# An expert layer whose rows are gathered pair by pair, with a longer weight ring and single buffers

## The chip, the cores and the metric

One core of one Trainium2 chip runs the whole program. The time is the device time of that core in microseconds; three runs are given and their median is used. Smaller is better.

## The reference

Two transformer-like blocks run one after the other on 256 tokens of width 1024. The change lies in the last part of the second block, a mixture of experts with 32 experts of inner width 256, two of them per token, and in the norm behind it:

```
g_logits = t @ w_rg + b_rg;  g_sel = argmax(g_logits)           # 4 groups
e_in = (t @ w_re + b_re) of the chosen group                    # 8 experts each
top_v, top_i = top_k(e_in, 2);  w_top = softmax(top_v) * g_w
act = silu(t @ w_gate[e]) * (t @ w_up[e]) * combine[t, e]
y = sum over e of act @ w_down[e];   h = h + y
out = rms_norm(h, norm_final)
```

The reference computes every expert for every token and multiplies by a combine weight that is zero for 30 of the 32. The kernel computes only the chosen ones.

## The kernel before

The program is written out by hand for each engine, and semaphores tie the engines together. The dense layers before the experts read 112 weight units of 1 MB (`raw`), which ScalarE and GpSimd split in a high and a low part (`whi`, `wlo`, lines 580 and 524); that part is as before. The last unit is the router's (`rt`, lines 2305 to 2313).

Behind the router, VectorE finds the two experts of each token and makes one-hot masks `oh` and their sum `msum` (line 1623). TensorE turns them into counts (`cn`) and positions (`ds`). The 512 choices (256 tokens, two each) are sorted by expert: a choice's position is its expert's offset plus its rank there. VectorE makes a 256x512 selection matrix `pick`, and TensorE gathers all 512 rows of the normed tokens at once, transposed, with the high and low parts `xnh` and `xnl` as stationaries (`xg`, lines 2341 to 2347). ScalarE copies them out as `xs`.

The experts' work is cut into tiles of TS = 32 positions of one expert. Two tiles make a pair. 16 pairs ("e") hold the first tile of each of the 32 experts, and 8 pairs ("o") can hold the tiles of experts with more than 32 choices; which experts these are is known at run time only. `pair_plan` (line 117) sets the order of the 24 pairs. For each pair GpSimd copies the two windows of `xs` into `xw` (line 547) and of the choice weights into `wx`. TensorE runs `gate_up` (line 2381: 32 matmuls with 32-column stationaries, four side by side on the array), two transposes of the gated product (`act_transposed`, line 2373), `down` (line 2400) and `combine` (line 2412), which adds each row back to its token in four PSUM banks that stay occupied through all pairs. ScalarE applies silu and copies the high part of y (`y_hi`), VectorE multiplies gate and up (`gate`), copies the activations (`act_copy`), makes the owner matrix `sT` (`owners`) and the low part of y (`y_lo`). Everything there is in two buffers, and the order on TensorE is gate_up(j), combine(j-2), down(j-1), with the transposes of pair j-1 in the middle of gate_up(j).

Expert weights come in units of 1 MB through a ring of NRING = 13 buffers. A pair needs six units: four for gate and up (part 0 and 1), two for down (part 2). SyncE issues them in the order of `ring_plan` (line 129). The first four go to memory that is free once the output projection of the mixer is done. The next nine wait for the last dense weights to be used (line 505). From then on each entry waits until the entry that held its buffer has been read (line 508). For an "o" pair the load is conditional and moves nothing when there is no such tile.

Of the kernel before, what the change touches and what calls it, by code (L numbers as in the profile page):

```python
# [34 lines left out]
NRING = 13  # L35
# [6 lines left out]
for _n, _w in (("ident", 128), ("tri", 128), ("stri", 128), ("ones", 128), ("cmpmask", 30), ("cos", 16), ("sin", 16),  # L42
               ("invf", 16), ("iota", 32), ("rcos", 128), ("rsin", 128), ("negmask", 128), ("slot", 1)):
    CONST[_n] = (sum(w for _, w in CONST.values()), _w)
# [72 lines left out]
def pair_plan():  # L117

    pairs = []
    for n in range(NEXP // 2):
        pairs.append(("e", n))
        if n % 2 == 0 and n or n == 3:
            pairs.append(("o", len(pairs) - n - 1))
    return pairs


def ring_plan(npair):


    ring = []
    for j in range(npair + 1):
        if j < npair:
            ring += [(j, part, u) for part in range(2) for u in range(2)]
        if j:
            ring += [(j - 1, 2, u) for u in range(2)]
    return ring


def bank_plan(units):
# [58 lines left out]
    G += [("xg", k) for k in range(8)]  # L200
# [24 lines left out]
    W += [("rtt", 0), ("cn", 0), ("ds", 0), ("wr", 0), ("pT", 0), ("od", 0)]  # L225
# [12 lines left out]
def program(nc, x_d, mem_d, pos_d, cst_d, sml_d, dec_d, npost_d, nfin_d, w_d, ew_d, out_d):  # L238
# [9 lines left out]
    NT = len(PAIRS)  # L248
    RING = ring_plan(NT)
    ENTRY = {u: n for n, u in enumerate(RING)}  # L250
    ctx = ExitStack()
    with ctx:
# [128 lines left out]
        xnh = at("xnh", A + 8 * KB, [P, TT, DM], f32r)  # L381
        xnl = at("xnl", A + 16 * KB, [P, TT, DM], f32r)
        pick = at("pick", A + 24 * KB, [P, TT, NSLOT], f32r)
        ramp = at("ramp", A + 28 * KB, [P, NSLOT])
        a = A + 30 * KB
        oh = at("oh", a, [P, 2, TT, 32])
        msum = at("msum", a + 512, [P, TT, 32])
        prod = at("prod", a + 768, [P, 2, TT, 32])
        cnt = at("cnt", a + 1280, [32, P])
        offn = at("offn", a + 1792, [P, 2, 32])  # L390
        row = at("row", a + 2048, [P, 8, 32])
        over = at("over", a + 3072, [P, 8, NOVER])
        posf = at("posf", a + 3584, [P, 4])
        start = at("start", a + 3616, [P, NEXP + NOVER], i32)
        mine = at("mine", a + 3840, [P, NPAIR])
        overi = at("overi", a + 4064, [P, 2, NOVER], i32)
        rtl = at("rtl", A + 38 * KB, [P, 8, TT * 36])
        lgt = at("lgt", A + 38 * KB + 2304, [36, S])
        flt = at("flt", A + 42240, [32, P])
        xw = at("xw", A + 42 * KB, [P, 2, 8, 2 * TS])  # L400
        sg = at("sg", A + 46 * KB, [P, 2, 256])

        yhl = at("yhl", A + 8 * KB, [P, 2, 2, 512], f32r)
        ac = at("ac", A + 28 * KB, [2 * TS, 2, 256])
        tally = at("tally", A, [P, 2, NEXP])
        match = at("match", A + 512, [P, NOVER, NEXP])
        mval = at("mval", A + 512 + 2 * KB, [P, NOVER, NEXP])
        vals = at("vals", A + 512 + 4 * KB, [P, 4, NEXP])
        aT = at("aT", A + 22 * KB, [P, 2, 4 * TS])
        nfin = at("nfin", A + 24 * KB, [P, DM])  # L410
        xs = at("xs", base + 9 * UW * 4, [P, 8, NSLOT])
        a = base + 9 * UW * 4 + 16 * KB
        posT = at("posT", a, [P, 2 * S])
        sT = at("sT", a + 2 * KB, [P, 2, S], f32r)
        wrow = at("wrow", a + 4 * KB, [P, NSLOT])
        wx = at("wx", a + 6 * KB, [P, 2, 2 * TS])
        wpick = at("wpick", a + 8 * KB, [P, TT, NSLOT])
        diag = at("diag", a + 12 * KB, [P, 4, P])
        wtmp = at("wtmp", a + 14 * KB, [P, NSLOT])
# [2112 lines left out]
```

## Time and profile before

| | |
|---|---|
| time, median of 3 runs | 1198.32 us (1196.86 to 1198.56) |
| the profiled execution | 1198.53 us |
| its span | 1196.7 us |
| TensorE matmul busy | 1023.9 us, 86% |
| VectorE, ScalarE, GpSimd busy | 619.5, 426.6, 612.6 us |
| gate/up matmuls (L2393), 1536 records | 103.6 us |
| down matmuls (L2409), 384 records | 49.0 us |
| combine matmuls (L2419), 96 records | 32.4 us |
| expert weight issues (L507, L515) | 144, of 1024 KB each |

The span runs from the first to the last instruction; the time of an execution includes what lies around it. A record is what the profiler writes for one pass of an instruction; a plain fp32 matmul has two, an fp32r one has one. Busy times of TensorE overlap from one record to the next, so that the pace of a stretch is read from start to start. The experts' stage is about the last 285 us. All times below are counted from the start of the span.

### The profile page before, as it was taken

The page shows a single profiled execution, that of the slowest core. Times are in us where ns is not written, and L with a number is a line of the kernel's source. Part 1 is how long each engine was busy: PE and PEld are TensorE (multiplying, and loading weights), DVE is VectorE, ACT ScalarE, POOL GpSimd, SP SyncE. Part 2 cuts the span into 40 slices and gives each one's busy share as a digit, 9 for nine tenths or more (in the row PEclk, how much of TensorE's full clock was granted, in tenths as well). Part 3 has the DMA queues.
Part 4 walks back from the last instruction along what each step waited for, and adds up shares of the span by engine and source line. Part 5 has one row for each costly group of instructions (what it writes and reads, how often), then busy time and mean ns, then how long its engine had stood idle before and what let it go on. Part 6 is the DMA issues. An engine that isn't in the chain of part 4 may idle for free.

```text
span 1196.7 us, 19506 instructions
## 1 busy us (share of the span) xinstructions
PE 1023.9 (86%) x7452; PEld 840.0 (70%) x7452; DVE 619.5 (52%) x1343; ACT 426.6 (36%) x637; POOL 612.6 (51%) x549
## 2 busy tenths in 40 slices
PE   5897899987957979999999999999985879787773
PEld 4786788987946869999977789898964534333331
DVE  6303246368545665554159986842116656444445
ACT  4543333332224545554434344344432311111111
POOL 5997814456748676664765349888540011110100
PEclk9999898999987889999999999999996879999996
DMA  6554522333334344332433226554434589999990
GB/s 251 172 204 160 192 71 71 100 131 123 140 107 141 139 143 141 139 121 96 145 137 106 97 81 211 176 172 170 155 138 189 234 340 413 420 421 420 420 398 36
DMA packets 31907, 224.90 MB, mean 188 GB/s; under 512 B 3664, under 2 KB 3664, under 8 KB 5072
## 3 DMA queue, kind: packets, MB, share of 16 engines
q1 hardware_dynamic: 30672, 220.07, 48.9%
q10 hardware_dynamic: 1152, 3.67, 0.9%
q8 instruction: 59, 0.97, 0.3%
q14 instruction: 24, 0.20, 0.0%
HBM read 273.01 MB, written 1.05 MB: 229 GB/s over the span
## 4 chain that ended last, share of the span: by engine, by line
POOL 44%; issue 31%; DMA 12%; PE 9%; DVE 3%; SPq 0%; ACT 0%; POOLq 0%; DVEq 0%
POOL wlo L524 44%; DMA ring<-in_experts 12%; PE ps L2393 3%; PE ps L2409 1%; PE ps L2419 1%; DVE yhl L1720 1%; PE ps L2345 0%; PE ps L2346 0%; PE ps L1807 0%; PE ps L1809 0%; PE ps L1808 0%; PE ps L2378 0%; POOLq L527 0%; DVE x L1782 0%; SPq L507 0%
## 5 line engine op out<-in xcount | busy, mean ns | idle before, releaser
L524 POOL TENSOR_TENSOR wlo<-raw,whi 128x512 fp32r<-128x512 f32 x448 | 583.6, 1336 | 308.4 <-ACT whi L580 307.9
L1857 PE MATMUL ps<-xhi,whi 128*128 128x256 f32 x960 | 283.6, 295 | 10.5 <-DVE xlo L1210 4.1
L1858 PE MATMUL ps<-xhi,wlo 128*128 128x256 f32 x960 | 277.7, 289 | 0.0
L1859 PE MATMUL ps<-xlo,whi 128*128 128x256 f32 x960 | 277.4, 289 | 0.0
L580 ACT ACTIVATE whi<-raw 128x2048 fp32r<-128x2048 f32 x112 | 214.0, 1914 | 147.0 <-PE ps L1859 75.2
L1857 PEld LDWEIGHTS ps<-xhi,whi 128*128 128x128 f32 x960 | 191.0, 199 | 14.7 <-issue 7.1
L1858 PEld LDWEIGHTS ps<-xhi,wlo 128*128 128x128 f32 x960 | 190.6, 199 | 1.0 <-issue 0.7
L1859 PEld LDWEIGHTS ps<-xlo,whi 128*128 128x128 f32 x960 | 190.4, 198 | 0.0
L2393 PE MATMUL ps<-ring,xw 128*32 128x256 f32 x1536 | 103.6, 407 | 33.0 <-DMA ring<-in_experts 32.3
L1807 PE MATMUL ps<-whi,xhi 128*128 128x512 f32 (+3 forms) x298 | 117.8, 395 | 13.1 <-POOL wlo L524 11.1
L547 POOL COPY xw<-xs 128x256 f32 x48 | 20.4, 452 | 209.9 <-PE ps L2393 162.7
L1808 PE MATMUL ps<-wlo,xhi 128*128 128x512 f32 (+3 forms) x298 | 114.9, 386 | 0.0
L1809 PE MATMUL ps<-whi,xlo 128*128 128x512 f32 (+3 forms) x298 | 114.6, 385 | 0.0
L2393 PEld LDWEIGHTS ps<-ring,xw 128*32 128x32 f32 x1536 | 52.7, 114 | 77.3 <-issue 58.3
L1720 DVE TENSOR_TENSOR yhl<-ps,yhl 32x512 fp32r<-32x512 f32 x96 | 65.9, 687 | 75.9 <-ACT yhl L910 74.8
L1807 PEld LDWEIGHTS ps<-whi,xhi 128*128 128x128 f32 x298 | 57.6, 193 | 26.6 <-POOL wlo L524 10.5
L1808 PEld LDWEIGHTS ps<-wlo,xhi 128*128 128x128 f32 x298 | 57.6, 193 | 10.7 <-issue 1.0
L1809 PEld LDWEIGHTS ps<-whi,xlo 128*128 128x128 f32 x298 | 57.6, 193 | 10.3
L1150 DVE TENSOR_REDUCE stat<-ps 128x1 f32<-128x128 f32 (+1 forms) x36 | 11.0, 306 | 90.0 <-PE ps L1918 69.7
L2409 PE MATMUL ps<-ring,aT 128*32 128x512 f32 x384 | 49.0, 629 | 9.6 <-issue 6.8
L903 ACT ACTIVATE sg<-ps 128x256 f32<-128x256 f32 x24 | 9.2, 384 | 119.2 <-PE ps L2393 119.2
L658 ACT ACTIVATE pr<-ps,stat 128x128 f32<-128x128 f32 x64 | 26.2, 415 | 55.8 <-DVE stat L1151 55.8
(465 smaller groups left out, 1496.0 us busy)
## 6 DMA issues: line engine op xcount, KB each, us to landing
ring<-in_experts SPq DMA_DIRECT2D x144, 1024.0 KB
raw<-in_weights SPq DMA_DIRECT2D x112, 1024.0 KB, 4.9
x<-in_x SPq DMA_DIRECT2D x2, 512.0 KB, 4.5
memt<-in_mem ACTq DMA_DIRECT2D x1, 1024.0 KB, 6.0
out<-xn ACTq DMA_DIRECT2D x4, 256.0 KB, 2.5
decay<-in_decay ACTq DMA_DIRECT2D x1, 512.0 KB, 4.1
npost<-in_norm_post ACTq DMA_DIRECT2D x1, 512.0 KB, 5.4
nfin<-in_norm_final ACTq DMA_DIRECT2D x1, 512.0 KB, 8.1
```

What stands on the lines that cost most here:

```text
L524: ins = pool.tensor_tensor(wlo[:, j, c], raw[:, j, c], whi[:, j, c].bitcast(f32), ALU.subtract)
L580: act.activation(whi[:, n % NSPL, :], raw[:, n % NRAW, :], ACT.Copy).then_inc(hi_ready, 1)
L658: ins = act.activation(p_buf[:, c], pj((S_, u))[:, c], ACT.Exp, bias=stat[:, NMAX + k + t:NMAX + k + t + 1], accum_out=stat[:, sums + k + ...
L1720: ins = v.tensor_tensor(yhl[other, j % 2, b, :], ps[3][own, :], yhl[own, j % 2, b, :].bitcast(f32), ALU.subtract)
L1807: mm(out, lh, rh, start=first, stop=False, skip_group_check=skip)
L1808: mm(out, lh, rl, start=False, stop=False, skip_group_check=skip)
L1809: return mm(out, ll, rh, start=False, stop=last, skip_group_check=skip)
L1857: mm(o_, wh[:, k, cc], hi[:, k0 + r0 + k, :], start=first, stop=False, skip_group_check=True)
L1858: mm(o_, wl[:, k, cc], hi[:, k0 + r0 + k, :], start=False, stop=False, skip_group_check=True)
L1859: ins = mm(o_, wh[:, k, cc], lo[:, k0 + r0 + k, :], start=False, stop=last, skip_group_check=True)
L2393: ins = mm(ps[j % 2][q:q + TS, 0:256], xw[:, j % 2, 4 * part + k, TS * u:TS * u + TS], wt[u][:, k, 256 * h:256 * h + 256], start=first, st ...
L2409: ins = mm(ps[3][q:q + TS, :], aT[:, j % 2, 2 * TS * k + TS * u:2 * TS * k + TS * u + TS], wt[u][:, k, 512 * h:512 * h + 512], start=k == ...
```

## The change

1. Slots are numbered by expert and rank. The slot of a choice is 32 times its expert plus its rank; a choice of rank 32 or more goes to an overflow slot, which needs the tallies of all experts (`tally`) first. Pair 0 needs only the ranks.
2. The gather of all rows, `xs`, `xnh`, `xnl` and GpSimd's window copies go. Each pair has a `gather(j)` on TensorE: 16 fp32 matmuls with `xn` as stationary and a 256x64 selection `pick` as moving operand. VectorE makes the selection (`pick_rows`), and scales and copies the rows out (`rows_out`).
3. The choice weights are no longer applied to the activations. They are gathered once into `wslot`, a weight per slot and pair, and scale y on its way out of PSUM (`y_hi`, `y_lo`).
4. The ring has 18 buffers and a plain order, and each buffer of the dense layers is handed over by its own last reader.
5. The buffers of gate/up, transposes, `sg`, `ac`, `aT` and `yhl` are single. TensorE's order is gate_up(j), gather(j+1), transposes of j, combine(j-1), down(j).
6. The residual `x` is added by TensorE into the four combine banks (`residual_in`), once. The final squares read PSUM directly.
7. Two overflow pairs stand elsewhere in the order of pairs; there are still 24.

The diff, cut to its core:

```diff
-NRING = 13
+NRING = 18
@@ pair_plan
-        if n % 2 == 0 and n or n == 3:
+        if n in (3, 4, 5, 7, 9, 11, 13, 14):
@@ ring_plan
-    ring = []
-    for j in range(npair + 1):
-        if j < npair:
-            ring += [(j, part, u) for part in range(2) for u in range(2)]
-        if j:
-            ring += [(j - 1, 2, u) for u in range(2)]
-    return ring
+    return [(j, part, u) for j in range(npair) for part in range(3) for u in range(2)]
@@ ring buffers
+        slots = [A + (48 + 8 * i) * KB for i in range(4)]
+        slots += [base + 8 * KB * i for i in (1, 2, 0)]
+        slots += [base + 8 * KB * i for i in (4, 7, 5, 8)] + [base + 80 * KB, base + 96 * KB, A + 40 * KB]
+        slots += [base + 8 * KB * i for i in (3, 6)] + [base + 72 * KB, base + 88 * KB]
@@ SyncE
-                if n == 4:
+                if 4 <= n < 7:
+                    sp.wait_ge(lo_ready, NU - 6 + n)
+                if n == 7:
+                    sp.wait_ge(weights_used, NU - 1)
+                if n == 14:
                     sp.wait_ge(weights_used, NU)
@@ ScalarE
             for j in range(NT):
                 silu(j)
-                if j:
-                    y_hi(j - 1)
...
+                if j == 0:
+                    copy(("pT", 0), posT[:, :])
+                    wait_done(act, ("ws", 0))
+                y_hi(j)
@@ VectorE
+            def pick_rows(j, at_):
+                do(v.tensor_tensor(hit[:, :, :], C("iota").unsqueeze(1).to_broadcast([P, 4, 2 * TS]), ALL4(at_, 2 * TS), ALU.is_equal))
+                sync()
+                v.tensor_tensor(pick[:, j % 2, :, :], hit[:, 0:2, :], hit[:, 2:4, :], ALU.add).then_inc(sem("pick_ready"), 1)
+
+            def rows_out(j):
+                dve.wait_ge(sem("gathered"), j + 1)
+                v.tensor_tensor(xw[:, j % 2, :, :], ps[1][:, :].rearrange("p (k s) -> p k s", k=8),
+                                D("g_moe").unsqueeze(2).to_broadcast([P, 8, 2 * TS]), ALU.mult).then_inc(sem("rows_ready"), 1)
...
             for j in range(NT):
-                gate(j)
                 if j:
                     y_lo(j - 1)
-                owners(j)
+                gate(j)
+                if j + 1 < NT:
+                    rows_out(j + 1)
                 act_copy(j)
                 if j == 0:
-                    overflow()
+                    slot_weights()
+                    wait_full(dve, ("ws", 0))
+                    release(v.tensor_copy(wslot[:, :], pj(("ws", 0))[:, 0:NPAIR]), ("ws", 0))
+                    wait_done(dve, ("ws", 0))
+                    further()
+                    wait_done(dve, ("pT", 0))
+                owners(j)
+                if j + 2 < NT:
+                    pick_rows(j + 2, codes[:, PLACE[j + 2], :])
@@ TensorE
+            def gather(j):
+                pe.wait_ge(sem("pick_ready"), j + 1)
+                for k in range(8):
+                    for t in range(TT):
+                        ins = mm(ps[1][:, 2 * TS * k:2 * TS * k + 2 * TS], xn[:, t, k * P:k * P + P], pick[:, j % 2, t, :], start=t == 0, stop=t == 1)
+                ins.then_inc(sem("gathered"), 1)
...
-            gate_up(0)
-            for j in range(1, NT):
+            for j in range(NT):
                 gate_up(j)
-                if j >= 2:
-                    combine(j - 2)
-                down(j - 1)
-            act_transposed(NT - 1)
-            combine(NT - 2)
-            down(NT - 1)
+                if j == 0:
+                    code_rows()
+                if j + 1 < NT:
+                    gather(j + 1)
+                act_transposed(j)
+                if j == 0:
+                    weights_of_slots()
+                if j == 1:
+                    residual_in()
+                if j:
+                    combine(j - 1)
+                down(j)
             combine(NT - 1)
```

How this moves instructions is seen in the order of each engine. First TensorE before, in the second half of the pairs: the end of one pair's gate/up (`ring_170`, `ring_171` are ring buffers) and what follows it.

```order
L2393 MATMUL ps<-ring_170,xw 32x256 [waits ring_loaded12,ring_loaded11]
L2378 MATMUL ps<-cst,ac 128x64 [waits aT_ready,gated]
L2378 MATMUL ps<-cst,ac 128x64
L2393 MATMUL ps<-ring_170,xw 32x256 x2
L2393 MATMUL ps<-ring_171,xw 32x256 x2
L2419 MATMUL ps<-yhl,sT 128x512 [waits y_lo_ready,owners_ready]
L2419 MATMUL ps<-yhl,sT 128x512 x3
L2409 MATMUL ps<-ring_159,aT 32x512 [waits aT_ready,y_lo_ready,ring_loaded1,ring_loaded0]
```

The same place in the changed kernel, where L2349 is gate/up, L2293 the gather, L2336 the transposes, L2377 combine and L2361 down:

```order
L2349 MATMUL ps<-ring_168,xw 32x256 x2
L2349 MATMUL ps<-ring_169,xw 32x256 x2
L2293 MATMUL ps<-pick,xn 128x64 [waits pick_ready]
L2293 MATMUL ps<-pick,xn 128x64 x15
L2336 MATMUL ps<-cst,ac 128x64 [waits gated]
L2336 MATMUL ps<-cst,ac 128x64
L2377 MATMUL ps<-yhl,sT 128x512 [waits y_lo_ready,owners_ready]
L2377 MATMUL ps<-yhl,sT 128x512 x3
L2361 MATMUL ps<-ring_170,aT 32x512 [waits aT_ready,ring_loaded17,ring_loaded16]
```

The transposes belonged to the pair before and stood inside gate/up; now they are the pair's own, and 16 full-width matmuls stand ahead of them. Down is that of the same pair, no longer of the one before.

SyncE's queue where the ring is first filled, before (every row is one unit; rows without a wait follow at once, four, nine and then one by one):

```order
L507 DMA ring_159<-in_experts 128x2048 [waits weights_used]
L507 DMA ring_163<-in_experts 128x2048 [waits weights_used]
L507 DMA ring_159<-in_experts 128x2048 [waits first_used]
L507 DMA ring_160<-in_experts 128x2048 [waits first_used]
L507 DMA ring_161<-in_experts 128x2048 [waits gu_full]
```

And now:

```order
L511 DMA ring_154<-in_experts 128x2048 [waits weights_used]
L511 DMA ring_158<-in_experts 128x2048 [waits lo_ready]
L511 DMA ring_161<-in_experts 128x2048 [waits weights_used]
L511 DMA ring_168<-in_experts 128x2048 [waits weights_used]
L511 DMA ring_154<-in_experts 128x2048 [waits first_used]
L511 DMA ring_156<-in_experts 128x2048 [waits gu_full]
L511 DMA ring_158<-in_experts 128x2048 [waits y_full]
```

Four units go on the first wait, three on a wait each for the splits, seven on the next and four on the last before reuse begins with the nineteenth.

VectorE between the slot weights of pair 0 and the low part of its y, in the changed kernel; `which_slot` feeds the matmuls of `weights_of_slots`, `mval`, `match` and `over` are the overflow table, `pick` is what gather(2) waits for:

```order
L1702 TENSOR_TENSOR which_slot<-islot,choice 128x512 [waits islot_ready]
L1705 COPY which_pair<-which_pair 128x4 [waits which_ready,dve_step]
L1734 COPY wslot<-ps 128x24 [waits bank_full6]
L1711 TENSOR_TENSOR mval<-cst,tally 128x512 [waits bank_done6]
L1713 TENSOR_TENSOR match<-mval,tally 128x512 [waits dve_step]
L1715 SCALAR_TENSOR_TENSOR match<-mval,match 128x512 [waits dve_step]
L1717 TENSOR_REDUCE over<-match 128x16 [waits dve_step]
L1669 TENSOR_SCALAR own<-posT,cst 128x512 [waits bank_done5]
L1671 TENSOR_TENSOR sT<-own 128x256 [waits dve_step]
L1599 TENSOR_TENSOR pick<-hit 128x128 [waits dve_step]
L1678 SCALAR_TENSOR_TENSOR yhl<-ps,wslot,yhl 32x512 [waits y_hi_ready]
```

Before, the overflow table stood between the activations' copy of pair 0 and the gate of pair 1, and nothing of the next rows hung on VectorE.

## Rows read from the trace of the kernel before

**Rows 1.** Stretches: length; busy PE PEld DVE ACT POOL; PEclk, DMA share, GB/s.
```profile
890.00:900.00 10.00, 10.00 (x43) 8.19 (x42) 4.19 (x13) 1.15 (x2) 2.47 (x2) 0.93 0.00 0
920.00:930.00 10.00, 6.88 (x23) 5.94 (x23) 6.38 (x27) 0.69 (x1) 0.00 (x0) 0.50 1.01 425
950.00:960.00 10.00, 4.19 (x66) 2.05 (x54) 9.40 (x27) 0.97 (x2) 1.04 (x4) 0.81 0.18 75
1130.00:1140.00 10.00, 6.96 (x62) 3.04 (x66) 2.80 (x7) 0.46 (x2) 1.04 (x4) 0.83 1.01 419
613.90:616.00 2.10, 2.10 (x19) 2.04 (x18) 0.00 (x0) 0.60 (x1) 1.91 (x2) 1.00 0.60 254
```

**Rows 2.** The weights' DMA queue: packets, MB, share of 16 engines.
```profile
q1 hardware_dynamic: 30672, 220.07, 48.9%
```

**Rows 3.** SyncE in order of time: start us, us, what.
```profile
912.48 32.15 SPq L507 DMA_DIRECT2D ring<-in_experts  x12
```

**Rows 4.** Waits from 965 to 1166 us: total us, times, longest.
```profile
PE ps L2393 <- DMA ring<-in_experts: 32.3, 18, 3.0
```

**Rows 5.** TensorE in order of time, one pair: start us, us, instruction, records.
```profile
984.06 1.20 PE L2419 MATMUL ps<-yhl,sT 128*128 128x512 f32 x4
985.19 1.93 PE L2409 MATMUL ps<-ring,aT 128*32 128x512 f32 x16
986.93 2.77 PE L2393 MATMUL ps<-ring,xw 128*32 128x256 f32 x48
989.63 0.33 PE L2378 MATMUL ps<-cst,ac 64*128 64x64 f32 x2
989.90 1.07 PE L2393 MATMUL ps<-ring,xw 128*32 128x256 f32 x16
991.23 0.47 PE L2419 MATMUL ps<-yhl,sT 128*128 128x512 f32 x1 [0.26 <-DVE yhl L1720]
```

**Rows 6.** TensorE in order of time, in the scan.
```profile
614.00 1.89 PE L2226 MATMUL ps<-xtok,segM 128*128 128x64 f32 x16
615.73 0.65 PE L2209 MATMUL ps<-segR,cst 128*128 128x512 f32 x1
```

**Rows 7.** The chain that ended last, from router to pair 0: start us, us.
```profile
919.08 1.06 PE ps L2327 x4
...
921.13 0.85 PE ps L2334 x4
...
926.52 0.77 PE ps L2345
927.29 0.43 PE ps L2346
...
932.64 0.23 PE ps L2345
...
940.59 0.42 PE ps L2393 x3
```

**Rows 8.** VectorE in order of time, positions of the choices.
```profile
923.44 0.29 DVE L1628 TENSOR_TENSOR prod<-oh,ps 128x128 f32<-128x128 f32 x1 [2.98 <-PE ps L2337]
```

**Rows 9.** Groups of VectorE from 900 us on: busy us, mean ns, idle before.
```profile
L1720 DVE TENSOR_TENSOR yhl<-ps,yhl 32x512 fp32r<-32x512 f32 x96 | 65.9, 687 | 75.9 <-ACT yhl L910 74.8
L1695 DVE TENSOR_TENSOR ac<-sg,ps 32x256 f32<-32x256 f32 x48 | 20.1, 418 | 25.2 <-ACT sg L903 24.5
L1752 DVE TENSOR_TENSOR mval<-match,vals 128x512 f32<-128x512 f32 x3 | 2.1, 689 | 0.1
```

**Rows 10.** The chain's last part: last y, last combine, first residual adds.
```profile
1178.73 0.60 ACT yhl L909
1179.33 0.50 ACT yhl L910
...
1182.79 2.06 PE ps L2419 x4
1184.87 2.48 DVE x L1782 x4
```

More of the change, by code:

```diff
@@ L248, in program @@
     NT = len(PAIRS)
+    PLACE = [n + NEXP // 2 * (kind == "o") for kind, n in PAIRS]
     RING = ring_plan(NT)
@@ L412, in program @@
[L412 to L419, printed above, removed]
-        ring = [at(f"ring{i}", A + (48 + 8 * i) * KB if i < 4 else base + (i - 4) * UW * 4, [P, UW])[:, :] for i in range(NRING)]
+        a = [A + 8 * KB]
@@ new lines, in small @@
+        def small(name, shape, dt=f32):
+            size = (4 * int(np.prod(shape[1:])) + 31) // 32 * 32
+            if a[0] <= A + 40 * KB < a[0] + size:
+                a[0] = A + 80 * KB
+            t = at(name, a[0], shape, dt)
+            a[0] += size
+            return t
+        rtl = small("rtl", [P, 8, TT * 36])
+        lgt = at("lgt", a[0], [36, S])
+        sg = small("sg", [P, 256])
+        yhl = small("yhl", [P, 2, 512], f32r)
+        oh = small("oh", [P, 2, TT, NEXP])
+        msum = small("msum", [P, TT, NEXP])
@@ new lines, in program @@
+        upto = small("upto", [P, 4, NPAIR + 1])
+        which_pair = small("which_pair", [P, 4, NPAIR])
+        which_slot = at("which_slot", a[0], [P, 4, P])
+        sT = small("sT", [P, 2, S], f32r)
+        islot = small("islot", [P, P])
+        diag = at("diag", a[0], [P, 4, P])
+        own = small("own", [P, 2 * S])
+        wslot = small("wslot", [P, NPAIR])
+        hit = small("hit", [P, 4, 2 * TS])
+        pick = small("pick", [P, 2, TT, 2 * TS])
+        posT = small("posT", [P, 2 * S])
@@ L885, in _ @@
             hi_parts("m", 8, 0, D("g_moe"))
-            for t in range(TT):
-                act.activation(xnh[:, t, :], xn[:, t, :], ACT.Copy).then_inc(sem("xnh_ready"), 1)
             act.wait_ge(sem("router_arg"), 1)
@@ new lines, in _ @@
+            do(v.tensor_scalar(flt[:, :], cnt[:, :], float(TS), None, ALU.is_gt))
+            for q in range(2, NSTEP + 1):
+                sync()
+                ins = v.scalar_tensor_tensor(flt[:, :], cnt[:, :], float(TS * q), flt[:, :], ALU.is_gt, ALU.add)
+                if q < NSTEP:
+                    do(ins)
+            ins.then_inc(sem("more_ready"), 1)
+            rows_out(0)
+            wait_full(dve, ("od", 0))
+            release(v.tensor_copy(tally[:, :, :], pj(("od", 0))[:, 0:64].rearrange("p (a e) -> p a e", a=2)), ("od", 0))
```

367 lines of the change are left out of this document (133 added, 234 removed).

## The prediction

> **What bounds the kernel now.** I read the table of stretches first. While the last dense layers run (890 to 900 us) no byte moves; at 920 to 930 the expert weights come at full rate, at 950 to 960 at 75 GB/s, and at 1130 to 1140 the DMA share is 1.01 at 419 GB/s with TensorE 0.70 busy [rows 1]. The weight queue carried 220.07 MB [rows 2]: 112 dense units and 96 expert units of 1.0486 MB are 218.1 of it. So only the 16 pairs of own tiles move weights; the 8 overflow pairs move none, but TensorE computes all 24 alike. A unit at 419 GB/s takes 2.5 us, a pair of six 15.0. Four units are fetched early, the next when the router's weights are read, at 912.5 us [rows 3]. From 965 to 1166 us TensorE waits 32.3 us for ring slots [rows 4]. Last, one pair whose weights were in time, TensorE alone [rows 5], from start to start: combine 1.13 us, down 1.74, 48 gate/up records 2.70, transposes 0.27, 16 more records 1.33 of which 0.26 is a wait: 6.91 without it. 24 x 6.91 = 166 us of TensorE stand against 16 x 15.0 = 240 us of DMA. The DMA bounds this stage, and TensorE has 74 us to spare.
>
> **The DMA side of the change** gets better. Entries 4 to 6 go out when the last splits are done, 7 to 13 when the last dense unit but the router's has been read, about 900 us, 14 to 17 at 912.5. Seven at 2.5 us from 900 are in by 917.5, four more by 927.5: the first three pairs. This moves the end only as long as the DMA bounds.
>
> **The TensorE side** gets worse. The gather of all rows at once (32 fp32r matmuls of 512 columns, 926.5 to 936.8 us) goes, and each pair gets 16 fp32 matmuls with a 128x128 stationary and 64 moving columns. An fp32 matmul is two records here (a pair's 32 gate/up matmuls show as 48 + 16). The scan has the same form: 16 records start at 614.00 us, the next group at 615.73 [rows 6], at clock 1.00 [rows 1]: 0.108 us a record. A gather is 32 x 0.108 = 3.46 us, a pair 6.91 + 3.46 = 10.4, and 24 pairs 249 us. That is more than 240 us of weights of which more come early, so TensorE becomes the bound.
>
> By the Trainium skill, "TensorE: Matmul & The Clock Gate", the section on LDWEIGHTS, a load costs by its columns, some 107 ns for 128; the row's 0.108 agrees, and the sum would be the same.
>
> Does the gather cover anything? It stands where the transposes wait for silu and gate, some 1.5 us. The old order covered those with the next pair's gate/up, so nothing is won.
>
> Do the other engines keep up, with each buffer single now? Counted from the end of a down: ACT's two y_hi end at +1.2 [rows 10], DVE's four y_lo of 0.69 [rows 9] at +4.1. Gate/up ends at +3.6, silu at +4.1, the gates (2 x 0.42 [rows 9]) at +5.0, the gather at +7.1. After it rows_out (0.69, the 128x512 form [rows 9]) and the copy (0.29, the 128x128 form [rows 8]) end at +8.2, while TensorE does transposes and combine until +8.5. So the transposes have 2.1 us of slack and down 0.3. Owners (0.69 at most + 0.4) and pick (0.4 + 0.3) end at +10.0, before the next gather. Scaling y_hi by the slot's weight I cost at nothing. For y_lo the scaled form is not in the trace: from 0.69 (same size) to twice that, and even 5.5 us would end under the gather. POOL's window copies go; they were off the path.
>
> Do weights come late? The ring now reaches three pairs ahead, at most two of them with weights after the fourth pair: 30.0 us of transfer against 3 x 10.4 = 31.2 of TensorE. The 32.3 us of waits go. SP's conditional issues stand in the order of their releases, and nothing queues up behind them.
>
> **The front**, in the old trace's clock. The expert choice is there at 919.1. The four records of L2331 and L2332 took 0.99 (from 919.08 + 1.06 to 921.13 [rows 7]); now they are first: 920.1. DVE: product and reduction 0.29 each [rows 8], three small steps of 0.2, hit and pick 0.7: 922.1. Gather 0 begins cold: a record of a full stationary took 0.85 / 4 = 0.21 then, and the old gather went from 0.43 to 0.23 a record 5.9 us after its start [rows 7]. With about 5 us at 0.21 and the rest at 0.108: 6.2 us, 928.4. Rows_out and hops: gate/up of pair 0 starts at 929.3 in place of 940.6 [rows 7], 11.3 us earlier. Gate/up 3.7, code rows (8 records) 0.9, gather 3.5, transposes 0.3: 937.8. DVE: rows_out and copy 1.0, then the slots' weights, a dozen small steps and one of 0.69: 942.0, for which TensorE waits 4 us at the head of its queue with down 0 and pair 1 behind. Eight records 0.9, down 1.7: 944.7. DVE meanwhile makes the overflow table, six steps at 0.72 [rows 9] and a cast: 947.9; owners 0, pick 2: 949.7. Gate/up 1 is done at 948.4, gather 2 waits for that pick: 953.2; transposes 953.5; the residual is 4 fp32 matmuls of 512 columns, 8 records at 0.43 (down's pace, 1.74 for 4 groups [rows 5]), 3.5: 957.0; combine and down: 959.9. At half the clock after the 4 us wait, down 0 and gate/up 1 could cost up to 4 more, of which 1.3 lie beside the wait for the pick. I take 1.6: gate/up of pair 2 starts at 961.5.
>
> **The sum.** 21 x 10.4 = 218.4: gate/up of the last pair starts at 1179.9. There no gather covers the gate: 3.7 + 0.5 + 0.9, transposes 0.4, combine 1.1, down 1.9, y_hi 1.2, y_lo 2.8, last combine 1.9 (2.06 before [rows 10]): 14.4, so 1194.3. The old end of that combine is 1182.79 + 2.06 = 1184.85, and 11.85 us follow up to 1196.7. Of these, the residual adds of the first half leave (2 x 0.65), its squares are read from PSUM in two (2 x 0.7 for 1.25) and a small add of 0.2 comes: 11.0 with the hops. Span 1205.3, 8.6 us longer. The profiled execution took 1198.53 us for its span of 1196.7, and the median is 1198.32, the same within 0.02%. With the same 1.8 around it: **1207 us**.
>
> **Bounds.** A gather record: from 0.054 (64 columns at down's pace, 1.74 / 4 for 512) to 0.118 (the 1.89 us busy for the 16 records, with the last one's latency [rows 6]): 1.7 to 3.8 us a gather. I take 0.108, start to start, the identical form. Changes between tiled and full stationary: 0 to 0.2 a pair. Pair 2's start: 957 to 965.
>
> **Rivals.**
> A. The gather's loads hide behind other work. At 0.054 a record a pair is 8.6 us on TensorE, three pairs 26 against 30 of weights, and the DMA bounds again: 12 pairs x 15.0 = 180 us from the release in pair 2 at about 964, then 14.4 + 11.0, some 3 us of waits and the 1.8: 1174. Halfway, at 9.5 a pair, it is 21 x 0.9 = 19 us less than forecast: 1188. For it: in gate/up (48 records in 2.70 us) four records with narrow stationaries already share the array. Against it: the scan's row, where 16 full stationaries stand in line at 0.108 each. It decides from 9.9 us a pair, a gather of under 2.9. Chance 0.20.
> The skill's section on the back-to-back issue gap (same page) gives 81 ns per matmul of 128 columns with loads; by that a gather is 2.6 us and the time near 1188, on this rival's side. The row of 0.108 speaks against it.
> B. The single buffers don't fit: ps0 holds gate/up and transposes, ps1 the gather, yhl one tile. If down waits 1 us in each pair for the copy behind rows_out: +21, 1228. For it: only 0.3 us of slack there. Against: 2.1 us before the transposes, and all steps have rows. Chance 0.12.
> C. Pairs at 10.0 and a front at 960: 1198, no change. 0.10.
> D. The forecast, 10.1 to 10.8 a pair: 1201 to 1216. 0.58.
> That it doesn't do what it says, and the DMA still bounds beside pairs of 10.4, is ruled out by 240 against 249 with the earlier start.
>
> 0.2% (2.4 us) is about what a measurement of this kernel tells from no change. Slower by more: D and B less their edge, 0.68. Same: C and that edge, 0.12. Faster: A, 0.20. The likeliest's own range is 1201 to 1216; with A's nearer half and the bounds 1187 to 1218.
>
> **What will show it.** TensorE's period in the second half 10.4 us, 3.5 of it 32 gather records; waits for the ring near zero; a DMA share under one between 960 and 1150. Pair 0's gate/up near 929, pair 2's near 961.5, a wait of 4 us before the weights of slots. It is wrong if gather records come at 0.08, if the DMA row stays at nine, or if transposes or down wait in each pair.

## The result, and the profile after

The changed kernel takes 1212.57 us (median of four runs, 1209.64 to 1213.43), against 1198.44 us of the kernel before, timed beside it on the same chip (1196.86 to 1200.69). The ratio is 1.0117 with a 95% interval of 1.0095 to 1.014: slower, by 14 us. The profiled execution took 1213.04 us, its span 1211.3 us, 14.6 longer than before.

First the stretches of the changed kernel, with the columns of [rows 1]:

```profile
890.00:900.00 10.00, 10.00 (x39) 8.10 (x38) 2.58 (x10) 1.15 (x2) 4.16 (x4) 0.86 0.62 211
920.00:930.00 10.00, 8.24 (x37) 7.68 (x38) 4.50 (x20) 1.49 (x2) 0.00 (x0) 0.50 1.02 426
960.00:1150.00 190.00, 190.00 (x2132) 127.53 (x2131) 110.12 (x214) 29.71 (x54) 0.00 (x0) 1.00 0.91 368
```

Expert weights now arrive beside the last dense layer (0.62 of the DMA engines at 890 to 900, where before there was nothing). In the pairs TensorE is busy 190 of 190 us at a granted clock of 1.00, where [rows 1] has 6.96 of 10 us at 0.83. TensorE now bounds this stage. The view of waits from 965 to 1190 us says the same. It has no row of TensorE waiting for the ring, against 32.3 us in [rows 4]. TensorE's only wait there, 1.9 us, is in the last pair. The DMA share over the same 190 us is 0.91, so the transfers are not far behind.

On the page, the chain that ended last has lost its DMA (12% before) and TensorE has grown from 9% to 23%:

```profile
POOL 43%; issue 30%; PE 23%; DVE 2%; ACT 0%; POOLq 0%; DVEq 0%
```

TensorE in order of time, for one pair of the changed kernel (columns as in [rows 5]; L2349 is gate/up, L2293 the gather, L2336 the transposes, L2377 the combine, L2361 the down matmuls):

```profile
1058.72 3.64 PE L2349 MATMUL ps<-ring,xw 128*32 128x256 f32 x64
1062.29 3.79 PE L2293 MATMUL ps<-pick,xn 128*128 128x64 f32 x32
1066.01 0.33 PE L2336 MATMUL ps<-cst,ac 64*128 64x64 f32 x2
1066.27 1.20 PE L2377 MATMUL ps<-yhl,sT 128*128 128x512 f32 x4
1067.39 1.92 PE L2361 MATMUL ps<-ring,aT 128*32 128x512 f32 x16
1069.13 3.64 PE L2349 MATMUL ps<-ring,xw 128*32 128x256 f32 x64
```

From one gate/up to the next it is 10.41 us. From start to start: gate/up 3.57, gather 3.72, transposes 0.26, combine 1.12, down 1.74. The gather's 32 records stand 0.116 us apart. In the old pair of [rows 5] the same work without the gather took 6.91 us.

The front, from the experts' choice to the gate/up of pair 2 (same view; L2298 makes the first counts, L2325 gathers the slots' weights):

```profile
920.70 0.69 PE L2298 MATMUL ps<-msum,cst 128*128 128x64 f32 x2 [5.75 <-DVE msum L1585]
...
923.81 7.06 PE L2293 MATMUL ps<-pick,xn 128*128 128x64 f32 x32 [1.06 <-DVE pick L1599]
...
931.79 6.32 PE L2349 MATMUL ps<-ring,xw 128*32 128x256 f32 x64
...
946.24 1.91 PE L2325 MATMUL ps<-which_pair,which_slot 128*128 128x24 f32 x8 [3.25 <-DVE which_pair L1705]
948.07 3.29 PE L2361 MATMUL ps<-ring,aT 128*32 128x512 f32 x16
951.19 3.63 PE L2349 MATMUL ps<-ring,xw 128*32 128x256 f32 x64
...
965.02 1.26 PE L2349 MATMUL ps<-ring,xw 128*32 128x256 f32 x20
```

Pair 0's gate/up starts at 931.79, 8.8 us earlier than in [rows 7], although the work up to the choice ended 1.6 us later in this execution (920.70 against 919.08). The gather, gate/up 0 and, after the 3.25 us wait, down 0 take longer than in a later pair: 7.0 us against 3.72, 6.3 against 3.57, 3.1 against 1.74. The granted clock of these three stretches is 0.50, 0.56 and 0.54.

The end, same view, from the last gate/up on:

```profile
1183.65 3.64 PE L2349 MATMUL ps<-ring,xw 128*32 128x256 f32 x64
1189.18 0.33 PE L2336 MATMUL ps<-cst,ac 64*128 64x64 f32 x2 [1.88 <-DVE ac L1660]
1189.44 1.78 PE L2377 MATMUL ps<-yhl,sT 128*128 128x512 f32 x4
1191.15 2.93 PE L2361 MATMUL ps<-ring,aT 128*32 128x512 f32 x16
1198.63 2.05 PE L2377 MATMUL ps<-yhl,sT 128*128 128x512 f32 x4 [4.55 <-DVE yhl L1678]
```

By the chain that ended last, the last of the four y_lo of the pair before ends at 1188.24, and the gate of the last pair starts behind it at 1188.27. The last combine ends at 1200.7 and 10.6 us follow. The low part of y in its scaled form takes 748 ns on average (groups of the page, as in [rows 9]), against 687. The trace of before doesn't have it at this size, but the same operation stands in its final norm, on 128x512 without an operand in PSUM, and took 748 ns there too (L1790), so the size could have been read ahead:

```profile
L1678 DVE SCALAR_TENSOR_TENSOR yhl<-ps,wslot,yhl 32x512 fp32r<-32x512 f32 x96 | 71.8, 748 | 57.5 <-ACT yhl L872 56.4
```

### The profile page after: what moved, and what is told of

Read it like the earlier page. It is cut to its first block, busy times and chain, and to the rows that moved or that the text cites. A ratio compares the mean times of both kernels' runs of the same rounds, so it can differ in the third digit from the quotient of the medians.

```text
span 1211.3 us, 20525 instructions
## 1 busy us (share of the span) xinstructions
PE 1093.2 (90%) x8190; PEld 920.5 (76%) x8190; DVE 639.8 (53%) x1390; ACT 423.3 (35%) x630; POOL 583.9 (48%) x453
## 4 chain that ended last, share of the span: by engine, by line
POOL 43%; issue 30%; PE 23%; DVE 2%; ACT 0%; POOLq 0%; DVEq 0%
POOL wlo L528 43%; PE ps L2293 8%; PE ps L2349 7%; PE ps L2361 4%; PE ps L2377 2%; PE ps L2336 1%; DVE yhl L1678 0%; PE ps L1769 0%; PE ps L1770 0%; PE ps L1771 0%; PE ps L2370 0%; POOLq L531 0%; DVE xn L1752 0%; DVE stat L927 0%; PE ps L2325 0%
## 5 line engine op out<-in xcount | busy, mean ns | idle before, releaser
L1819 PE MATMUL ps<-xhi,whi 128*128 128x256 f32 x960 | 283.9, 296 | 10.4 <-DVE xlo L1176 4.1
L1769 PE MATMUL ps<-whi,xhi 128*128 128x512 f32 (+3 forms) x298 | 118.2, 397 | 12.4 <-POOL wlo L528 10.4
L1678 DVE SCALAR_TENSOR_TENSOR yhl<-ps,wslot,yhl 32x512 fp32r<-32x512 f32 x96 | 71.8, 748 | 57.5 <-ACT yhl L872 56.4
L2293 PEld LDWEIGHTS ps<-pick,xn 128*128 128x128 f32 x768 | 90.8, 198 | 10.5 <-issue 10.1
L2293 PE MATMUL ps<-pick,xn 128*128 128x64 f32 x768 | 94.0, 282 | 1.1 <-DVE pick L1599 1.1
L2349 PE MATMUL ps<-ring,xw 128*32 128x256 f32 x1536 | 90.0, 387 | 0.0
L2349 PEld LDWEIGHTS ps<-ring,xw 128*32 128x32 f32 x1536 | 50.6, 112 | 45.1 <-issue 17.1
L871 ACT ACTIVATE yhl<-ps,wslot 128x512 fp32r<-128x512 f32 x24 | 16.6, 690 | 166.1 <-PE ps L2361 166.1
L2361 PE MATMUL ps<-ring,aT 128*32 128x512 f32 x384 | 48.5, 625 | 0.0
```

Of the source, the lines that this page charges most:

```text
L1678: ins = v.scalar_tensor_tensor(yhl[other, b, :], ps[3][mine, :], wslot[mine, PLACE[j]:PLACE[j] + 1], yhl[mine, b, :].bitcast(f32), ALU.mul ...
L1769: mm(out, lh, rh, start=first, stop=False, skip_group_check=skip)
L1819: mm(o_, wh[:, k, cc], hi[:, k0 + r0 + k, :], start=first, stop=False, skip_group_check=True)
L2293: ins = mm(ps[1][:, 2 * TS * k:2 * TS * k + 2 * TS], xn[:, t, k * P:k * P + P], pick[:, j % 2, t, :], start=t == 0, stop=t == 1)
L2349: ins = mm(ps[0][q:q + TS, 0:256], xw[:, j % 2, 4 * part + k, TS * u:TS * u + TS], wt[u][:, k, 256 * h:256 * h + 256], start=first, stop=last)
L2361: ins = mm(ps[3][q:q + TS, :], aT[:, 2 * TS * k + TS * u:2 * TS * k + TS * u + TS], wt[u][:, k, 512 * h:512 * h + 512], start=k == 0, stop ...
```

## The experiments

All ratios are to the kernel before, timed beside each run on the same chip. The changed kernel stands at 1.0117 by this measure. The runs are from several chips, so their ratios compare better than their medians. The theory to test: the gather's 3.7 us on TensorE in each of 24 pairs moved the bound from the DMA to TensorE, and the faster start gives part of it back. The rival: the single buffers and the new order set the pace whatever the gather costs.

**The gather cut to an eighth.** The gathers from pair 2 on make one block of eight (the rows of those pairs are stale):

```diff
-                for k in range(8):
+                for k in range(8 if j < 2 else 1):
```

> The changed kernel with the gathers of pairs 2 to 23 cut to one of their eight column blocks (4 records instead of 32; the other rows are stale, so this part of the computation is left out). All other instructions and waits stand. Theory 1 (TensorE bounds, and the gather is what put it there): from gate/up of pair 2 at 965 us a pair can fall from 10.41 us, but not by the whole 3.25: with the gather gone the chain of the single buffers shows, down, y_hi 1.3, y_lo 3.0, gate 0.9, transposes, combine, 8.5 us a pair. The DMA (12 pairs x 15.0 us) comes to nearly the same. 1176 us, from 1170 to 1182, with TensorE waiting some 1.5 us a pair for the gate. Rival 2 (the gather lies in the shadow of that chain): 1205 or more. Rival 3 (the DMA bound the changed kernel all along): unchanged, 1212.

Measured: 1208.23 us (1206.62 to 1210.78), ratio 1.0101 [1.0064, 1.0138]. The forecast of 1176 was missed by 32 us, and the time lies where rival 2 had it. TensorE's work went down by some 3 us a pair and the pair barely changed. Rival 3 is out: TensorE waited for no weights from 965 to 1160 us. TensorE in order of time:

```profile
1084.88 3.63 PE L2349 MATMUL ps<-ring,xw 128*32 128x256 f32 x64
...
1090.40 0.33 PE L2336 MATMUL ps<-cst,ac 64*128 64x64 f32 x2 [1.30 <-DVE ac L1660]
1090.66 1.60 PE L2377 MATMUL ps<-yhl,sT 128*128 128x512 f32 x4
1092.19 3.13 PE L2361 MATMUL ps<-ring,aT 128*32 128x512 f32 x16
1095.14 3.62 PE L2349 MATMUL ps<-ring,xw 128*32 128x256 f32 x64
```

A stretch of this run:

```profile
1100.00:1110.00 10.00, 8.96 (x90) 4.04 (x90) 5.92 (x12) 1.65 (x3) 0.00 (x0) 0.83 1.01 415
```

The period is 10.26 us, and the gather between (not shown) has 0.66 us for its four records. The transposes wait 1.30 us for the gate, and behind the wait combine takes 1.53 in place of 1.12 and down 2.95 in place of 1.74. The granted clock of such a stretch is 0.83; it is 1.00 in the changed kernel. So two things may have been hidden under the gather that the prediction had not priced: a chain through the single buffers, and the clock of the work behind a wait. This run alone doesn't say which of them makes the 10.26. The new theory is that the clock falls with the wait, and that more work on TensorE, if it fills enough of the wait, would make the pair shorter.

**The same gather in bf16.** ScalarE and GpSimd split the normed tokens once in two bf16 parts, and the gather is 32 single-pass matmuls, as many records as before (ring of 17 for the room). The selection `pick`, the moving operand, is bf16 as well:

```diff
-NRING = 18
+NRING = 17
+            for t in range(TT):
+                act.activation(xnb[:, 0, t, :], xn[:, t, :], ACT.Copy).then_inc(sem("xnb_hi"), 1)
...
+                    pool.tensor_tensor(xnb[:, 1, t, c], xn[:, t, c], xnb[:, 0, t, c], ALU.subtract).then_inc(sem("xnb_lo"), 1)
...
-                        ins = mm(ps[1][...], xn[:, t, k * P:k * P + P], pick[:, j % 2, t, :], start=t == 0, stop=t == 1)
+                        for b in range(2):
+                            ins = mm(ps[1][...], xnb[:, b, t, k * P:k * P + P], pick[:, j % 2, t, :], start=t == b == 0, stop=t == b == 1)
```

> The changed kernel with the gather in bf16: xn is split in a high and a low bf16 part (ScalarE, GpSimd), and a gather is 32 single bf16 matmuls of a 128x128 stationary and 64 columns in place of 16 fp32 ones with two records each; one ring buffer less (17) makes room. Theory 1 (a gather costs what its stationary loads cost, and a bf16 load is cheaper than the 0.11 us of fp32): at 0.06 us a record a gather is 1.9 us and a pair 8.6, 1178 (1172 to 1190). Rival (the pace is by record, whatever the type): 0.11 us a record, no change, 1212.

Measured: 1177.03 us (1172.55 to 1178.12), ratio 0.9827 [0.9785, 0.9869]: faster than both kernels. One pair on TensorE, in order of time:

```profile
1092.89 3.66 PE L2360 MATMUL ps<-ring,xw 128*32 128x256 f32 x64
1096.49 1.11 PE L2303 MATMUL ps<-pickb,xnb 128*128 128x64 bf16 x32
1098.42 0.33 PE L2347 MATMUL ps<-cst,ac 64*128 64x64 f32 x2 [0.83 <-DVE ac L1669]
1098.69 1.19 PE L2388 MATMUL ps<-yhl,sT 128*128 128x512 f32 x4
1099.81 1.92 PE L2372 MATMUL ps<-ring,aT 128*32 128x512 f32 x16
1101.55 3.64 PE L2360 MATMUL ps<-ring,xw 128*32 128x256 f32 x64
```

and VectorE's y_lo in the same pair, the gate right behind it:

```profile
1094.46 3.03 DVE L1687 SCALAR_TENSOR_TENSOR yhl<-ps,wslot,yhl 32x512 fp32r<-32x512 f32 x4 [2.35 <-ACT yhl L881]
```

The 32 records of the gather take 1.1 us (from 1096.49 to 1098.42 less the wait of 0.83), 0.034 a record, against 3.72. The period is 8.66 us, not 10.41 less 2.6: TensorE now waits 0.83 us, for a chain of which VectorE's row shows a part. From the end of down, y_hi runs to about 1094.4, y_lo to 1097.5, the gates to 1098.4, and then transposes, combine and down follow. That chain is 8.66 us long and is the new bound of the pair. The clock stays at 1.00. TensorE's waits from 965 to 1150 us (total us, times, longest):

```profile
PE ps L2347 <- DVE ac L1669: 15.8, 20, 0.8
PE ps L2360 <- DMA ring<-in_experts: 8.1, 4, 3.9
```

Weights are late in four places, so the DMA is near its bound as well.

**The bf16 gather, cut to an eighth** from pair 2 on (stale rows again), to part the clock from the chain: less work on TensorE than in the run before, the same chain of buffers.

```diff
-                for k in range(8):
+                for k in range(8 if j < 2 else 1):
```

> The bf16 gather kernel with the gathers of pairs 2 to 23 cut to one of eight column blocks (4 records of 32; the other rows are stale, so this part is left out). The period of 8.65 us is set by down, y_hi, y_lo, gate and transposes, so that TensorE loses 0.9 us of work per pair and waits 1.9 us in place of 0.84. Theory 4 (what held the fp32 kernel with cut gathers at 10.27 us a pair was TensorE's clock, granted at 0.84 on average, with combine and down at the lower level after the wait): the same here, less work and yet 10.2 us a pair, about 1206. Rival (the clock fell there for another reason, and the chain alone counts): 8.65 us a pair as with the whole gather, 1177.

Measured: 1200.85 us (1197.41 to 1203.18), ratio 1.0027 [1.001, 1.0043]: 24 us slower than the kernel that gathers in full. TensorE in order of time, and the stretch of one down:

```profile
1090.66 3.63 PE L2360 MATMUL ps<-ring,xw 128*32 128x256 f32 x64
...
1096.18 0.34 PE L2347 MATMUL ps<-cst,ac 64*128 64x64 f32 x2 [1.67 <-DVE ac L1669]
1096.44 1.81 PE L2388 MATMUL ps<-yhl,sT 128*128 128x512 f32 x4
1098.18 2.90 PE L2372 MATMUL ps<-ring,aT 128*32 128x512 f32 x16
1100.90 3.63 PE L2360 MATMUL ps<-ring,xw 128*32 128x256 f32 x64
```

```profile
1098.20:1100.80 2.60, 2.60 (x17) 0.69 (x20) 0.32 (x2) 0.00 (x0) 0.00 (x0) 0.62 1.01 422
```

The transposes start at the same point of the pair as in the full gather (5.52 us from the gate/up's start against 5.53), since the chain sets it. Behind it combine is 1.74 in place of 1.12 and down 2.72 in place of 1.74. The granted clock while down runs is 0.62; during gate/up (1090.66 to 1094.30) it is 1.00, and in the run before it is 1.00 during down too. These 1.6 us are the whole difference of the periods (10.24, from 1090.66 to 1100.90, against 8.66). So the clock theory holds: with a pause of 1.67 us in each pair much of the work behind it ran at the lower of the clock's two levels, with one of 0.83 it did not. Had the chain alone counted, the pair would have stayed at 8.66.

**Only the overflow pairs' gathers cut**, in fp32 (they have nothing to gather here):

```diff
-                for k in range(8):
+                for k in range(8 if PAIRS[j][0] == "e" else 1):
```

> The changed kernel (fp32 gather) with the gathers of the 8 overflow pairs cut to one of eight blocks; these pairs hold no tokens in this data. Theory 1 with the chain alone: an iteration whose gather is cut takes 8.5 us in place of 10.41, 8 x 1.9 = 15 us less, 1197. Theory 4 (the wait that appears lets the clock fall, and part of the pair then runs at 1.2 GHz): such an iteration takes 10 us or more, and the next one starts slow: under 4 us less, 1209 or even more than the whole kernel.

Measured: 1203.4 us (1197.95 to 1208.36), ratio 1.0051 [1.0032, 1.007], between the two theories. Two pairs with a cut gather, TensorE in order of time:

```profile
1050.90 0.33 PE L2336 MATMUL ps<-cst,ac 64*128 64x64 f32 x2 [1.29 <-DVE ac L1660]
...
1052.81 3.00 PE L2361 MATMUL ps<-ring,aT 128*32 128x512 f32 x16
...
1081.99 0.33 PE L2336 MATMUL ps<-cst,ac 64*128 64x64 f32 x2 [1.29 <-DVE ac L1660]
...
1083.37 1.92 PE L2361 MATMUL ps<-ring,aT 128*32 128x512 f32 x16
```

and the stretches behind the two waits:

```profile
1050.90:1055.60 4.70, 4.70 (x22) 1.75 (x26) 2.32 (x6) 0.00 (x0) 0.00 (x0) 0.64 1.01 425
1082.00:1085.00 3.00, 3.00 (x22) 1.41 (x26) 2.30 (x6) 0.00 (x0) 0.00 (x0) 1.00 1.01 423
```

The same wait of 1.29 us was followed once by a granted clock of 0.64 and a slow down, and once by 1.00 and the full pace. Of the eight cut gathers in this trace five went the first way, at 10.1 to 10.3 us a pair, and three the second, at 8.65. What decides between them at this length of wait is open. A cut is worth 1.8 us where the clock holds and some 0.15 where it falls, which gives about 6 us; the 21 pairs took 212.7 us against 218.6, 5.9 less. The rest of the 8.6 us by which the span is shorter is mostly the part before the choice, which ended 2.2 us earlier in this execution.

**The gather in one fp32r pass**, 16 records of the same shape (the part that rounding drops is left out of the rows), to price the record:

```diff
-NRING = 18
+NRING = 17
...
-        pick = small("pick", [P, 2, TT, 2 * TS])
+        pick = small("pick", [P, 2, TT, 2 * TS], f32r)
...
+            for t in range(TT):
+                act.activation(xnr[:, t, :], xn[:, t, :], ACT.Copy).then_inc(sem("xnr_ready"), 1)
...
-                        ins = mm(ps[1][...], xn[:, t, k * P:k * P + P], pick[:, j % 2, t, :], start=t == 0, stop=t == 1)
+                        ins = mm(ps[1][...], xnr[:, t, k * P:k * P + P], pick[:, j % 2, t, :], start=t == 0, stop=t == 1)
```

> The gather in one fp32r pass: ScalarE makes a copy of the normed tokens rounded to fp32r, and a gather is 16 matmuls of one record each with the same 128x128 stationary and 64 moving columns (the part that the rounding drops is left out of the rows; ring of 17). The fp32 gather took 3.72 us for 32 records, 0.116 each; the bf16 gather 1.02 us for 32 records, 0.032 each. Theory 1 (the price is that of a record with a 4-byte stationary of 128 columns, whatever the number of passes): 16 x 0.116 = 1.9 us a gather, TensorE without a pause before the transposes, clock 1.00, period 8.65 us as with bf16 since the chain down, y_hi, y_lo, gate sets it; time about 1177. Theory 2 (only the two-pass fp32 form is dear): 16 x 0.032 = 0.5 us a gather, a wait of about 1.3 us for the gate before the transposes, which is between the bf16 gather (0.84 us, clock 1.00) and the cut one (1.67 us, clock 0.83): either 8.65 us and 1177, or the clock falls in the pairs as in the cut gather, about 10.3 us a pair and 1200. The gather's own length separates the theories whatever the clock does.

Measured: 1178.03 us (1177.06 to 1181.04), ratio 0.9845 [0.9811, 0.9879]. TensorE in order of time:

```profile
1126.83 1.98 PE L2296 MATMUL ps<-pick,xnr 128*128 128x64 f32 x16
1128.79 0.33 PE L2340 MATMUL ps<-cst,ac 64*128 64x64 f32 x2
```

16 records take 1.96 us, 0.122 each: theory 1. The price is that of a pass with a 4-byte stationary of 128 columns, 0.12 us, and half the passes cost half. There is no wait before the transposes here: the gather fills the time to the gate, and the pair is 8.66 us (1123.27 to 1131.93) as in the bf16 run. TensorE waits 8.1 us for weights, as there. The groups of weight loads from 965 to 1150 us part the stationary from the rest (count, busy us, mean ns of one), fp32r here and bf16 in the run above:

```profile
L2296 PEld LDWEIGHTS ps<-pick,xnr 128*128 128x128 f32 x320 | 37.2, 191 | 8.2 <-issue 8.2
```

```profile
L2303 PEld LDWEIGHTS ps<-pickb,xnb 128*128 128x128 bf16 x640 | 19.8, 98 | 8.2 <-issue 8.2
```

Same tile, twice the loads and half the time. The moving operand is 64 columns in all three forms, but in bf16 its type changed too, so that run alone doesn't part the two. Combine does: it is an fp32r pass with the same 128x128 stationary, and takes 1.12 / 4 = 0.28 us a record for 512 moving columns, which is 0.035 for 64. The 4-byte gathers at 0.12 a record were not held by their columns. That leaves the load as what they paid for.

**The ring back to 13 buffers, all fetched late**, which undoes the DMA side of the change:

```diff
-NRING = 18
+NRING = 13
-                if 4 <= n < 7:
-                    sp.wait_ge(lo_ready, NU - 6 + n)
-                if n == 7:
-                    sp.wait_ge(weights_used, NU - 1)
-                if n == 14:
+                if n == 4:
                     sp.wait_ge(weights_used, NU)
```

> The changed kernel with the ring half undone: 13 ring buffers, and entries from the fifth on fetched only when the router's weights have been used. Theory 1 (TensorE at 10.4 us a pair bounds; weights have slack): no change, 1212 within 2, waits for the ring under 3 us. Rival (the longer ring and the early fetch are what keep the weights in time): waits for the ring come back, 5 buffers x 2.5 = 12 us or more later, 1224.

Measured: 1210.13 us (1207.2 to 1212.28), ratio 1.0104 [1.0064, 1.0144], no different from the changed kernel, and there is no wait for the ring from 965 to 1190 us. With TensorE as the bound the 18 buffers and the early fetch are worth nothing that can be measured.

**The early fetch in the kernel before**, which does that part alone where the DMA bounds (the order of the ring's buffers is changed with it, so that each goes where a dense buffer comes free):

```diff
-                if n == 4:
+                if 4 <= n < 7:
+                    sp.wait_ge(lo_ready, NU - 6 + n)
+                if n == 7:
+                    sp.wait_ge(weights_used, NU - 1)
+                if n == 11:
                     sp.wait_ge(weights_used, NU)
```

> The kernel before with the early fetch alone: its ring of 13 buffers is handed over buffer by buffer by the dense layers' last readers, so that 11 of 13 units are fetched before the router's weights are used. Theory (the ring was full at 937 us and its first buffer came free only at 942.6, when pair 0 had been started: what is fetched early only waits longer): no change, 1196 within 2. Rival (the idle transfer time at 890 to 912 us is what the DMA-bound stage lacks): up to 17 us less, 1180.

Measured: 1197.47 us (1192.01 to 1202.51), ratio 0.9988 [0.9963, 1.0013]. The stretches:

```profile
890.00:900.00 10.00, 9.77 (x45) 7.73 (x44) 4.93 (x14) 1.72 (x3) 0.82 (x1) 0.98 0.37 120
920.00:930.00 10.00, 6.89 (x25) 5.74 (x25) 7.49 (x29) 1.91 (x3) 0.00 (x0) 0.60 0.00 0
```

The transfers moved ahead and the DMA stood idle at 920 to 930 us instead, since 13 buffers were full and pair 0 had not begun. Filling a ring earlier gains nothing if the ring is full long before its first reader.

**The front in another order**: the weights of the slots ahead of the pairs, the third pick ahead of the overflow table.

```diff
+            slot_weights()
             for j in range(NT):
@@
                 if j == 0:
-                    slot_weights()
@@
-                    further()
                     wait_done(dve, ("pT", 0))
+                    pick_rows(2, codes[:, PLACE[2], :])
                 owners(j)
-                if j + 2 < NT:
+                if j == 0:
+                    further()
+                elif j + 2 < NT:
```

> The changed kernel with VectorE's slot weights moved ahead of the gate of pair 0, into the time in which it waits for gate/up, and the pick of pair 2 moved ahead of the overflow table. Theory 1: the 3.25 us wait of TensorE before the weights of slots goes, and what follows it on a path to the end moves with it: 3.5 us less (3 to 6, the more if the clock then doesn't fall in down 0), 1209. Rival: gather 2 waits instead, as the overflow table and y_lo of pair 0 are still to be done: under 1 us.

Measured: 1206.29 us (1205.2 to 1208.04), ratio 1.0079 [1.0051, 1.0107]. TensorE in order of time:

```profile
929.84 5.51 PE L2351 MATMUL ps<-ring,xw 128*32 128x256 f32 x64
...
940.15 1.07 PE L2327 MATMUL ps<-which_pair,which_slot 128*128 128x24 f32 x8
941.15 1.92 PE L2363 MATMUL ps<-ring,aT 128*32 128x512 f32 x16
...
957.97 3.64 PE L2351 MATMUL ps<-ring,xw 128*32 128x256 f32 x64
```

The wait of 3.25 us is gone and down 0 takes 1.74 us again in place of 3.1. From the first gate/up to the third it is 28.1 us against 33.2 in the changed kernel, 5.1 less; by the ratios (1.0079 against 1.0117) the whole is some 4.5 us shorter, by the medians 6.3. The 5.1 are the wait of 3.25, the 2.2 us of lower clock behind it (0.8 at the slots' weights, 1.4 at down 0) and 0.8 in gate/up 0, less a new wait of 1.15 before the transposes of pair 1, whose gate now stands behind the overflow table and y_lo of pair 0. So the rival had a part in it, a small one.

**Both together**, the bf16 gather and the front's order (the two diffs above):

> The bf16 gather and the moved slot weights together. With the bf16 gather a pair took 8.65 us and TensorE waited for weights only once, 4 us near 1110 us, so both sides are nearly level. Theory (chain of the single buffers and DMA nearly level): the front's 4 to 5 us are won on both sides, as the first releases of ring buffers come earlier too, of which up to half goes back as waits for weights: 1173 to 1175. Rival (the DMA bounds by now from its first byte): no gain over 1177.

Measured: 1169.85 us (1167.12 to 1175.45), ratio 0.9767 [0.9726, 0.9808]. It is the best of the versions, 2.3% under the kernel before, and 3 us under the forecast of 1173 to 1175. The part that was expected to go back as waits for weights did not. From 960 to 1150 us TensorE waited 17.4 us for the gate and 6.8 us for weights, so its pairs stand between the chain of single buffers and the DMA.

## Why the prediction was right, and where not

The forecast was 1207 us, slower; it is 1212.6. By its own steps:

**The bound and the waits: right.** TensorE took the place of the DMA, the 32.3 us of ring waits went, no engine held TensorE up from pair 2 on, and rival B (single buffers that don't fit) did not come about: neither the transposes nor down waited before the last pair.

The slack came out as reckoned: in the pair shown the gates end 1.8 us before the transposes start (2.1 forecast) and the copy 0.4 us before down (0.3). One of the signs of being wrong, a DMA row that stays at nine, did show: the page's row reads 8, 8, 9, 9, 9, 9 from 969 to 1151 us. It was too coarse a sign. Weights for 240 us of transfer stand beside 250 us of TensorE work, so the DMA is nearly always busy although nobody waits for it.

**The gather: nearly right in size, for the reason given.** 3.72 us against 3.46, and yet a pair of 10.41 against 10.4, since gate/up, in one piece now, took 3.57 where the 6.91 held 3.77 (2.70 and 1.33 less 0.26, [rows 5]). That the two errors cancel is luck. The 21 pairs took 218.6 us against 218.4. The row of the scan [rows 6] held. The back-to-back issue gap of the Trainium skill ("TensorE: Matmul & The Clock Gate"), 81 ns a matmul, on rival A's side, did not: a record was 0.116. The Trainium skill's rule on LDWEIGHTS (same page), some 107 ns for a load of 128 columns, comes within 15% of the 0.116 and 0.122 of the 4-byte passes; the bf16 records at 0.034 lie far below it.

**"Does the gather cover anything? ... nothing is won": wrong**, though it did not show in the forecast, because the gather of 3.72 us covered everything. The step counted the wait before the transposes as silu and gate, 1.5 us, and left it there. The step on the other engines had the gates end 5.0 us behind a down; with transposes, combine and down (3.1 us) that is a chain of 8.1 us a pair even without a gather, which was never added up. Measured it is 8.66, with the gates at +5.5, since y_hi and y_lo took longer. And where the pause is long, it costs twice, once as time and once as clock. So in the new order cutting a gather from 3.72 us to 0.66 brought 0.15 us a pair, and shortening it to 1.1 us brought 1.75. Rival A had nearly the right time by a sum that was half right: it gave 1174 with the DMA as the bound. With a gather of 1.1 us the kernel took 1177, and TensorE waited twice as long for the gate (15.8 us) as for weights (8.1).

**Scaling y_hi, "cost at nothing": a small miss.** ScalarE's two y_hi took 690 and 679 ns from 960 to 1190 us, against 597 and 592 without the scale before. It lies under the gather, and is part of the 8.66 where there is less of a gather.

**The front: mis-sized.** Gate/up of pair 2 came at 965.0 against 961.5. 1.6 of the 3.5 us were there before the experts' stage began, in an execution whose dense part was that much longer. The other 1.9 are several sizes that partly made up for each other. Gather 0 took 7.0 us against 6.2 (whose own terms, 5 us at 0.21 a record and the rest at 0.108, give 5.9) and gate/up 0 6.3 against 3.7: the sum had full clock there, and it was 0.56. The wait for the weights of slots was 3.25 us, where the steps gave 4.2, and gather 2 did not wait for its pick (1.3). The lower clock behind the wait cost 2.3 us, 0.9 at the slots' weights and 1.4 at down 0, where 1.6 was taken. The run with the front in another order bears this out from the other side.

**The last pair: mis-sized.** 17.0 us against 14.4. The gate began 0.4 later, because y_lo of pair 22 stood ahead of it with no gather to cover it. Behind the 1.88 us wait, transposes, combine and down took 4.98 us where 3.4 was forecast, at a granted clock of 0.64. The scaled y_lo at 0.75 us added 0.2, and y_hi, the last combine and the hops between them 0.4. The tail was 10.6 against 11.0.

In sum the span is 6.0 us over the forecast, and with rounding these are 1.6 of the dense part, 1.9 of the front, 0.2 of the pairs and 2.6 of the last pair, less 0.4 of the tail. The first is not the change's. Three of the experiments have the same program up to there (the fp32 gather cut to an eighth, only the overflow pairs' gathers cut, and the front in another order until its choice), and began the choice at 916.84, 918.45 and 918.75, where the changed kernel began it at 920.70.

**What stays open.** Why the clock fell behind five waits of 1.29 us and not behind three others was not settled. Nor is it known how short a gather can be before the clock falls; in every pair, 1.1 and 1.96 us went with full clock, 0.3 and 0.66 us with a clock of 0.83.

## What to carry to other kernels

Where a change takes time from the transfers and gives it to TensorE, add up both per tile before anything else: 16 x 15.0 against 24 x 10.4 decided this one. The small gather here was paid by the load of its 4-byte stationary, not by its 64 columns, so look at the type of the stationary first. And before taking work away from TensorE, add up the chain that it covers and look at the clock behind the pause that it leaves: cutting the bf16 gather to an eighth moved the ratio from 0.983 to 1.003.

## What the runs showed of the hardware

- With a pause of 1.30 or 1.67 us before the transposes of every pair, TensorE showed a granted clock of 0.83 to 0.84 over stretches of 10 us, 1.00 during gate/up and 0.58 and 0.62 while down ran. With one of 0.83 us in the same place it showed 1.00 throughout. Eight single pauses of 1.29 us among full pairs were followed by the lower clock five times and by 1.00 three times.
- A pass with a 4-byte 128x128 stationary and 64 moving columns took 0.116 us (fp32) and 0.122 us (fp32r) from start to start, one with stationary and moving operand in bf16 0.034 us. The loads themselves had a mean of 191 against 98 ns.
- A product of a PSUM operand with a per-partition weight, less a second operand, took 748 ns on VectorE for 32x512, against 687 for the subtraction alone [rows 9]. On ScalarE a copy of 128x512 from PSUM took 690 ns with a per-partition scale, against 597 without.
